# Attention bias added by VectorE out of PSUM, instead of six PE products a head

## What is computed

```python
q, k, v = jnp.split(h @ w_qkv, 3, axis=-1)
# per head, with q as 256 rows
s_own = jnp.einsum('hqd,hkd->hqk', qq, k_own) * scale
dist_own = t[:, None] - (own * B_BLOCK + key_off)[None, :]
s_own = jnp.where((dist_own >= 0)[None],
                  s_own + table_hb[h3, t5_bucket(dist_own)], -jnp.inf)
p = jax.nn.softmax(scores, axis=-1)
out = jnp.einsum('hqk,hkd->hqd', p_own, v_own)
```

## Time and profile before

| what | value |
|---|---|
| median of 3 runs | 1198.73 us (1198.47 to 1199.32) |
| profiled execution, its own time | 1199.04 us |
| its span, first to last instruction | 1197.1 us |
| mean granted TensorE clock | 0.997 |
| busy: PE, DVE, ACT, POOL | 98%, 66%, 56%, 2% |

### The profile page before, as it was taken

One profiled execution on the slowest core, in us unless ns is written; L12 is line 12 of the kernel. 1 busy time (PEld: TensorE's weight loads), 2 busy tenths in 40 slices (PEclk: granted clock), 3 DMA queues, 4 the chain that ended last, 5 costly groups with the idle time before them and its releaser, 6 DMA issues.

```text
span 1197.1 us, 17229 instructions
## 1 busy us (share of the span) xinstructions
PE 1173.2 (98%) x6884; PEld 1038.2 (87%) x6884; DVE 791.3 (66%) x803; ACT 673.4 (56%) x793; POOL 25.9 (2%) x28
## 2 busy tenths in 40 slices
PE   6999999999999999999998999999999999999998
PEld 5999998888889989888887888888898999888886
DVE  6787777655657556755655875656688777755663
ACT  6955675554455444544454754455687567454453
POOL 3000000000001000000000000000000000000000
PEclk9999999999999999999999999999999999999999
DMA  9543335645456434555644545646444333555450
GB/s 348 167 141 106 106 109 180 244 171 199 151 214 212 141 106 169 199 195 177 217 167 141 211 176 200 215 147 210 141 141 142 106 106 109 183 205 208 162 206 35
DMA packets 85128, 202.38 MB, mean 169 GB/s; under 512 B 3293, under 2 KB 5415, under 8 KB 84816
## 3 DMA queue, kind: packets, MB, share of 16 engines
q1 hardware_dynamic: 85040, 201.58, 48.8%
q0 software_dynamic: 32, 0.02, 0.0%
HBM read 200.52 MB, written 1.06 MB: 168 GB/s over the span
## 4 chain that ended last, share of the span: by engine, by line
PE 92%; ACT 3%; DVE 2%; issue 1%; POOL 1%; DMA 1%; SPq 0%; DVEq 0%; ACTq 0%
PE misc L615 10%; PE hb L615 10%; PE acc L667 10%; PE acc L668 10%; PE acc L669 10%; PE hb L620 5%; PE misc L620 5%; PE hb L542 4%; PE hb L543 4%; PE hb L540 4%; PE acc L778 2%; PE hb L557 2%; PE hb L555 2%; PE hb L556 2%; PE acc L766 1%; PE acc L767 1%
## 5 line engine op out<-in xcount | busy, mean ns | idle before, releaser
L1412 DVE TENSOR_TENSOR wlo<-raw,whi 128x2048 fp32r<-128x2048 f32 x186 | 423.4, 2304 | 163.9 <-ACT whi L1032 163.7
L1032 ACT ACTIVATE whi<-raw 128x2048 fp32r<-128x2048 f32 x186 | 348.3, 1906 | 117.5 <-PE acc L669 101.1
L667 PE MATMUL acc<-whi,arena_r 128*128 128x512 f32 x512 | 199.9, 390 | 0.0
L668 PE MATMUL acc<-wlo,arena_r 128*128 128x512 f32 x512 | 199.5, 390 | 0.0
L669 PE MATMUL acc<-whi,arena_r 128*128 128x512 f32 x512 | 199.2, 389 | 0.0
L615 PE MATMUL misc<-xhl,whi 128*128 128x512 f32 x512 | 122.7, 390 | 1.4 <-DVE arena L1863 1.4
L615 PE MATMUL hb<-xhl,whi 128*128 128x512 f32 x512 | 122.7, 390 | 0.0
L615 PEld LDWEIGHTS misc<-xhl,whi 128*128 128x128 f32 x512 | 95.3, 188 | 21.4 <-DVE arena L1863 2.0
L669 PEld LDWEIGHTS acc<-whi,arena_r 128*128 128x128 f32 x512 | 96.1, 188 | 20.2
L667 PEld LDWEIGHTS acc<-whi,arena_r 128*128 128x128 f32 x512 | 96.2, 188 | 19.1
L668 PEld LDWEIGHTS acc<-wlo,arena_r 128*128 128x128 f32 x512 | 96.2, 188 | 18.9
(11 more groups left out here) (263 smaller groups left out, 1810.5 us busy)
## 6 DMA issues: line engine op xcount, KB each, us to landing
raw<-in_mlp_w_dram SPq DMA_DIRECT2D x128, 1024.0 KB, 5.3
raw<-in_a_w_in_dram SPq DMA_DIRECT2D x32, 1024.0 KB, 5.8
raw<-in_b_w_qkv_dram SPq DMA_DIRECT2D x12, 1024.0 KB, 7.4
raw<-in_a_w_out_dram SPq DMA_DIRECT2D x8, 1024.0 KB, 5.1
raw<-in_b_w_out_dram SPq DMA_DIRECT2D x4, 1024.0 KB, 5.1
arena<-in_x_dram SPq DMA_DIRECT2D x2, 512.0 KB, 4.7
arena<-in_decay_dram SPq DMA_DIRECT2D x1, 1024.0 KB, 11.9
arena<-bias_rows SPq DMA_DIRECT2D x1, 1024.0 KB, 6.9
```

What stands on the lines that cost most here:

```text
L667: pe.matmul(o, ys, h, start=first and kt == 0, stop=False, skip_group_check=True)
L668: pe.matmul(o, ys, l, start=False, stop=False, skip_group_check=True)
L1032: act.activation(whi[:, g % 2, u, 0:n], raw[:, g % 2, u, 0:n], ACT.Copy).then_inc(hi_done, 1)
L1412: dve.tensor_tensor(wlo[:, g % 2, u, 0:n], raw[:, g % 2, u, 0:n], whi[:, g % 2, u, 0:n].bitcast(F32), ALU.subtract).then_inc(lo_done, 1)
```

## The change

The bias is no longer multiplied in. DVE adds it while it moves the scores from PSUM to `probs`, and maxima and exponentials then read `probs` in SBUF. The six products a head, `bh`, `bl`, the flip and the identity in fp32r go, with POOL's three instructions and DVE's and ACT's one each that made them. The bias row becomes 1024 long: the row as before, and the same row reversed ahead of it, so a second DVE copy. SP reads three tables of 128x128 a head (two through the row, one through the reversed part; rows of 512 bytes) where it read one of 128x256 (rows of 1 KB): two for the outer thirds of the scores, which DVE reads backwards, and one for the middle third, placed in `hn` (hence a wait for the norm's column sums). PE's `s_step(h)` waits for DVE's adds of head h-2 where it waited for ACT's exponentials, and ACT's wait for `p_mm` moves to DVE.

```diff
-        bias = carve(6144, HEADS, SEQ)
-        bh = arena_r[:, 0:2048].rearrange("p (a b) -> p a b", a=HEADS)
-        bl = arena_r[:, 2048:4096].rearrange("p (a b) -> p a b", a=HEADS)
+        bias_back = carve(6144, HEADS, 2, P)
+        bias_own = hn[:, 0:4, :].rearrange("p a (b x) -> p (a b) x", b=2)
...
                         sp.wait_ge(bias_out, 16)
-                        sp.dma_start(bias, bass.AP(tensor=bias_dram.tensor, offset=0,
-                                                   ap=[[1, P], [2 * SEQ, HEADS], [1, SEQ]])).then_inc(bias_in, 16)
+                        sp.wait_ge(ms_mm, mix_norm(layer) + 1)
+                        for to, first in ((bias_back[:, :, 0, :], SEQ - P + 1), (bias_back[:, :, 1, :], 2 * SEQ + P),
+                                          (bias_own, 2 * SEQ)):
+                            sp.dma_start(to, bass.AP(tensor=bias_dram.tensor, offset=first,
+                                                     ap=[[1, P], [4 * SEQ, HEADS], [1, P]])).then_inc(bias_in, 16)
...
-                        if h == 0:
-                            pe.wait_ge(bl_done, 1)
                         if h >= 2:
-                            pe.wait_ge(sexp, 2 * (h - 1))
-                        pe.matmul(s[:, 0:P], flip[:, :], bh[:, h, P:SEQ], start=True, stop=False)
-                        pe.matmul(s[:, 0:P], flip[:, :], bl[:, h, P:SEQ], start=False, stop=False)
-                        pe.matmul(s[:, 0:P], qT[:, h, 0:P], kT[:, h, 0:P], start=False, stop=True)
...
+                            pe.wait_ge(s_read, h - 1)
+                        pe.matmul(s[:, 0:P], qT[:, h, 0:P], kT[:, h, 0:P], start=True, stop=True)
+                        mm = pe.matmul(s[:, P:3 * P], qT[:, h, P:SEQ], kT[:, h, :], start=True, stop=True,
                                        skip_group_check=True)
...
                     def softmax(h):
                         act.wait_ge(smax, h + 1)
-                        if h >= 2:
-                            act.wait_ge(p_mm, h - 1)
...
-                            ins = act.activation(probs[:, h % 2, cs], acc[h % 2][:, cs], ACT.Exp,
+                            ins = act.activation(probs[:, h % 2, cs], probs[:, h % 2, cs], ACT.Exp,
...
-                        if k == 2:
-                            act.wait_ge(bias_in, 16)
-                            act.activation(bh, bias, ACT.Copy).then_inc(bh_done, 1)
...
-            dve.wait_ge(pool_const, 6)
+            dve.wait_ge(pool_const, 4)
...
-                    ch.did(dve.tensor_copy(bias_row, acc[2][0:HEADS, :]), bias_row_sb)
+                    ch.did(dve.tensor_copy(bias_row[:, 2 * SEQ:4 * SEQ], acc[2][0:HEADS, :]))
+                    ch.did(dve.tensor_copy(bias_row[:, 0:2 * SEQ], acc[2][0:HEADS, ::-1]), bias_row_sb)
...
                         if h >= 2:
+                            dve.wait_ge(p_mm, h - 1)
+                        ch.settle()
+                        if h == 0:
+                            dve.wait_ge(bias_in, 16 * 3)
+                        for_outer = [w.rearrange("p (c x) -> p c x", c=3)[:, 0:3:2, :]
+                                     for w in (probs[:, h % 2, :], acc[h % 2][:, 0:3 * P])]
+                        ch.did(dve.tensor_tensor(for_outer[0], for_outer[1], bias_back[:, h, :, ::-1], ALU.add))
+                        ch.did(dve.tensor_tensor(probs[:, h % 2, P:2 * P], acc[h % 2][:, P:2 * P], bias_own[:, h, :], ALU.add),
+                               s_read)
+                        if h >= 2:
                             dve.wait_ge(sexp, 2 * (h - 1))
-                            ch.settle()
-                        ch.did(dve.tensor_reduce(small[:, k:k + 1], acc[h % 2][:, 0:P], AX.X, ALU.max))
-                        ch.did(dve.tensor_reduce(small[:, k + 1:k + 2], acc[h % 2][:, P:3 * P], AX.X, ALU.max))
+                        ch.settle()
+                        ch.did(dve.tensor_reduce(small[:, k:k + 1], probs[:, h % 2, 0:P], AX.X, ALU.max))
+                        ch.did(dve.tensor_reduce(small[:, k + 1:k + 2], probs[:, h % 2, P:3 * P], AX.X, ALU.max))
...
-                        if k == 2:
-                            dve.wait_ge(bh_done, 1)
-                            ch.did(dve.tensor_tensor(bl, bias, bh.bitcast(F32), ALU.subtract), bl_done)
```

More of the change, by code:

```diff
@@ L188, in build_decoder @@
         tab = sb("tab", [BUCKETS + 1, HEADS])
-        flip = sb("flip", [P, P], F32R)
-        ident_r = sb("ident_r", [P, P], F32R)
         def carve(at, *dims):
@@ L239, in halves @@
                            ap=[list(flat.ap[0]), [2 * m, 256 // m], [step, 2], [1, m]])
-        bias = carve(6144, HEADS, SEQ)
-        bh = arena_r[:, 0:2048].rearrange("p (a b) -> p a b", a=HEADS)
-        bl = arena_r[:, 2048:4096].rearrange("p (a b) -> p a b", a=HEADS)
+        bias_back = carve(6144, HEADS, 2, P)
+        bias_own = hn[:, 0:4, :].rearrange("p a (b x) -> p (a b) x", b=2)
         probs = carve(8192, 2, 3 * P)
         pT = carve(9216, HEADS, 3 * P)
-        flip_in = carve(12416, P)
-        bias_row = arena[0:HEADS, 12288:12800]
+        bias_row = arena[0:HEADS, 11776:12800]
         gain_rows = arena[0:74, 12288:12288 + P]
@@ L269, in build_decoder @@
         misc = [misc_pair[:, i, :] for i in range(2)]
-        bias_dram = nc.dram_tensor("bias_rows", [HEADS, 2 * SEQ], F32, kind="Internal").ap()
+        bias_dram = nc.dram_tensor("bias_rows", [HEADS, 4 * SEQ], F32, kind="Internal").ap()
         raw_in = [[sem(f"raw_in{p}{u}") for u in range(2)] for p in range(2)]
@@ L300, in build_decoder @@
             sem("ol_done"))
-        bias_row_mm, bias_row_sb, bias_out, bias_in, bh_done, bl_done = (
-            sem("bias_row_mm"), sem("bias_row_sb"), sem("bias_out"), sem("bias_in"), sem("bh_done"), sem("bl_done"))
+        bias_row_mm, bias_row_sb, bias_out, bias_in, s_read = (
+            sem("bias_row_mm"), sem("bias_row_sb"), sem("bias_out"), sem("bias_in"), sem("s_read"))
         s_mm, smax, sexp, sscaled, p_mm, p_sb = (sem("s_mm"), sem("smax"), sem("sexp"), sem("sscaled"),
@@ L883, in _ @@
                     pe.wait_ge(tab_in, 32)
-                    pe.wait_ge(pool_const, 6)
+                    pe.wait_ge(pool_const, 4)
                     pe.wait_ge(y_sb, 4 * (layer - 1) + 3)
@@ L890, in s_step @@
                         pe.wait_ge(bank_free, free_count(layer) + 4 * (h // 4 + 1))
-                        if h == 0:
-                            pe.wait_ge(bl_done, 1)
                         if h >= 2:
-                            pe.wait_ge(sexp, 2 * (h - 1))
-                        pe.matmul(s[:, 0:P], flip[:, :], bh[:, h, P:SEQ], start=True, stop=False)
-                        pe.matmul(s[:, 0:P], flip[:, :], bl[:, h, P:SEQ], start=False, stop=False)
-                        pe.matmul(s[:, 0:P], qT[:, h, 0:P], kT[:, h, 0:P], start=False, stop=True)
-                        own = slice(SEQ - 1, P - 1, -1)
-                        pe.matmul(s[:, P:2 * P], ident_r[:, :], bh[:, h, 0:P], start=True, stop=False,
-                                  skip_group_check=True)
-                        pe.matmul(s[:, P:2 * P], ident_r[:, :], bl[:, h, 0:P], start=False, stop=False,
-                                  skip_group_check=True)
-                        pe.matmul(s[:, 2 * P:3 * P], ident_r[:, :], bh[:, h, own], start=False, stop=False,
-                                  skip_group_check=True)
-                        pe.matmul(s[:, 2 * P:3 * P], ident_r[:, :], bl[:, h, own], start=False, stop=False,
-                                  skip_group_check=True)
-                        mm = pe.matmul(s[:, P:3 * P], qT[:, h, P:SEQ], kT[:, h, :], start=False, stop=True,
+                            pe.wait_ge(s_read, h - 1)
+                        pe.matmul(s[:, 0:P], qT[:, h, 0:P], kT[:, h, 0:P], start=True, stop=True)
+                        mm = pe.matmul(s[:, P:3 * P], qT[:, h, P:SEQ], kT[:, h, :], start=True, stop=True,
                                        skip_group_check=True)
@@ L1933, in _ @@
             ch.settle()
-            ch.did(pool.memset(flip_in, 0.0))
-            ch.settle()
             ch.did(pool.affine_select(out=ident[:, :], in_=ident[:, :], compare_op=ALU.not_equal, fill=1.0, base=0,
@@ L1943, in _ @@
             ch.did(pool.memset(tab[BUCKETS:BUCKETS + 1, :], MASKED), pool_const)
-            ch.settle()
-            ch.did(pool.affine_select(out=flip_in, in_=flip_in, compare_op=ALU.not_equal, fill=1.0, base=1 - P,
-                                      pattern=[[1, P]], channel_multiplier=1))
-            ch.settle()
-            ch.did(pool.tensor_copy(flip[:, :], flip_in), pool_const)
-            ch.did(pool.tensor_copy(ident_r[:, :], ident[:, :]), pool_const)
             def sum_squares(n):
```

## The result

| | before | after |
|---|---|---|
| median, same chip | 1199.03 us (1198.47 to 1199.35, 4 runs) | 1206.93 us (1206.47 to 1207.31, 4 runs) |
| ratio after / before | | 1.0064, 95% interval 1.0052 to 1.0077 |
| profiled execution, its span | 1199.04, 1197.1 us | 1206.47, 1204.4 us |
| mean granted TensorE clock | 0.997 | 0.993 |

The kernel became 0.64% slower, past the upper end of the range (1201.0). Lines have moved in the changed kernel: ACT's split is L1018, VectorE's L1393, the adds L1742 and L1743, maxima L1748 and L1749, exponentials L1266, the copy of the transposes L1272, scores L892 and L893, transposes L902, SP's loads L403 and its table reads L432.

What follows compares the result with a forecast made beforehand. PE, busy 98% of the span, bounds the kernel; after the change the ACT and DVE chain binds attention. -2.0 us (chain) + 1.5 (clock) = -0.5: 1198.5 us for the profiled execution, median 1198.2, range 1195.0 to 1201.0.

Steps and rivals of the forecast that it cites:

- The three loads: SP's table reads before attention: cost the weight unit behind them 3.5 us, landing at 377.7, still hidden.
- The slower rival: The tables' packets delay group 3's first unit; 1201.0 us at the packets' bound; chance 0.18.
- two more issues of 0.37 us: On SP's queue, the added table loads' issues only queue behind data still moving; cost put at nothing.
- past 378.68 each microsecond would delay the whole chain: At ACT's split of group 3's first unit: later landing delays early maxima and, after 0.3 us slack, the chain.
- the clock: After PE's 2.8 us wait near the attention stage's end, a lower granted clock costs 1.5 us, bounds 0 and 1.7.
- the chain becomes the bound: In attention, ACT and DVE's loop takes 6.96 us a head against PE's 6.6 to 6.8; gain 2.0 us.
- The choice of no change for reductions: DVE's maxima cost the same from SBUF as from PSUM; the other bound saved 0.07 us on each of two.
- The second rival: Chain bound with the clock kept: 1196.7 us (1195.8 to 1197.1); chance 0.13.
- what comes off PE: Six bias products a head in attention: 0.60 us, at most 0.66; 4.8 us over eight heads.
- It doesn't stall PE at first: In attention PE runs on despite the slower chain, and the lag collects at the end as a 2.8 us wait.

Runs made afterwards that it cites:

- Experiment 5: The changed kernel with neighbouring heads' bias rows 2 KB apart in DRAM instead of 4 KB, still three table loads: 1200.25 us, ratio 1.0011.
- Experiment 6: The kernel before with its heads 4 KB apart in DRAM instead of 2 KB, nothing else: 1200.39 us, ratio 1.0012.
- experiments 3: The changed kernel with all table reads aligned (partition step 0 in DRAM, bias wrong): 1207.2 us, ratio 1.0072.
- experiment 4: The changed kernel with the three table loads issued from ACT's queue instead of SP's: 1203.4 us, ratio 1.0035.
- experiment 2: The kernel before with its one table load cut into two of 512 B rows, same bytes: 1198.94 us, ratio 0.9999.
- experiment 9: The changed kernel, heads still 4 KB apart, with VectorE's adds and maxima put ahead of its weight split: 1195.68 us, ratio 0.9973.
- experiment 8: The changed kernel with heads 2 KB apart and VectorE's adds and maxima put ahead of its weight split: 1193.77 us, ratio 0.9957.
- experiment 1: The changed kernel loading only the middle table, which all adds read (bias wrong): 1199.59 us, ratio 1.0004.
- experiment 7: The changed kernel with only the middle table (bias wrong), plus 15 filler products on PE before the last transposes: 1197.09 us, ratio 0.9984.
- 10: The changed kernel, heads 2 KB apart, maxima ahead of the split, table reads issued between group 3's two weight units: 1194.28 us, ratio 0.9959.

## Why the prediction was wrong

**The step that failed is "The three loads".** Their cost to the unit behind was put at 3.5 us, with 1.9 and 7.6 as bounds; it was 10.6. The slower rival, given 0.18, thus had the mechanism and its threshold right, and the size wrong. Experiment 5 has everything of the change but the distance between heads: its unit landed at 379.9, 5.7 us later than before, inside the bounds. The other 5 us came from the distance, which the prediction did not look at: it read bytes, rows and alignment off the diff and passed over `2 * SEQ` turning into `4 * SEQ`. Experiment 6 shows that term without the rest (the unit takes 2.7 us longer), experiments 3 and 5 together rule out alignment, and experiment 4 rules out that only SP's held-up issue was at fault. That issue, 3.38 us where two took 0.99, was missed as well: "two more issues of 0.37 us". So was 0.4 us for the write: twice as long, it landed 2.3 us after its issue instead of 1.9, and SP issued the reads at 365.15 instead of 364.70. Why rows 4 KB apart move at half the rate is not shown by these runs.

By the Trainium skill (DMA: Bandwidth & Descriptors, Specifications) rows of 512 B would have gone by bytes. The measurement decides against it for these overlapping reads of a small region: 74 to 86 GB/s at 4 KB between heads and 174 to 179 at 2 KB, while the 1 KB rows of before, with the unit behind them, moved at 246 to 349. At 2 KB experiment 2 comes close to it all the same, with 1.3 us for twice the rows.

**What the lateness cost was the order's doing.** The prediction said that past 378.68 each microsecond would delay the whole chain. That held: 6.2 us late at the split, and head 7's sums were read at 440.14 instead of the forecast's 433.75, 6.4 us late. With 1.1 us more for the clock than forecast (below), that makes 7.5 of the 8.0 us between the forecast for the profiled execution, 1198.5, and its 1206.47; the rest is not attributed. But the prediction took VectorE's order as given. Experiments 9 and 8 show the other half: with the maxima ahead of the split, the 4 KB between heads cost 1.8 us, 1.1 of them PE's wait for the late unit in experiment 9's trace, instead of 6.5 (the changed kernel against experiment 5).

**Right: the chain becomes the bound.** Forecast 6.96 us a head, measured 6.98 (experiments 1 and 7, and the changed kernel); adds 0.42 and 0.28, the maxima at 128 and 256 elements 0.29 and 0.41 from SBUF. The choice of no change for reductions was the right end: by the Trainium skill (VectorE: DVE Perf Modes, section on the TRN2 errata) they should have cost less each, an estimate of 0.07 us from its fixed parts, and these rows show none of it. Without the extra loads and with the clock kept the gain was 1.7 us (experiment 7: 1197.09 against 1198.83), forecast 2.0 with 1.7 as the lower bound. The second rival, chain bound and clock kept, was priced at 1196.7 (1195.8 to 1197.1), and this kernel is its case, at the upper end.

**Right, at its bound: what comes off PE.** In the changed kernel the scores of heads 0 and 1 stand 6.41 us apart, against 7.07: 0.66, the upper bound, not 0.60. Where PE is the slower party nearly all of it comes through: 8 x 0.66 = 5.3 us, and experiment 8 gains 5.1. The 0.5 us beyond the forecast's 4.8 also lengthen PE's wait where the chain binds: 3.5 us in experiment 1, forecast 2.8.

**Wrong size: the clock.** Forecast 1.5 us with 1.7 as the upper bound, measured 2.2 by the medians and 2.6 by the traces (experiment 1 against 7). In experiment 1 the rows read 0.78, 0.50 and 0.59 over 9 us, a longer stretch than the 4 and 3 us of the earlier trace rows on which the bound stood. So even with the loads priced well the sum would have come out above before, as experiment 1 did by 0.4, not 0.5 below.

**Missed: the bank.** "It doesn't stall PE at first" held only while the lag was under the 2.2 us of slack between the emptying of the projection bank and head 4's scores. In the changed kernel PE stopped there for 2.71 us, and the clock was low from 414 to 417. The projections that followed were not the slower party then, and the next copy came 7.19 us after the last instead of 6.98, so it cost 0.2 us; it was a second sign of the same lag, not a second cause.

The balance in the two profiles: the last copy of the stage ended at 442.35 instead of 437.69, 4.7 us later, and from there to ACT's last rounding of the outputs it took 8.3 us instead of 5.7 (450.68 and 443.40), 2.6 more, with the clock low: together the 7.3 us between the spans.

## What to carry to other kernels

Before pricing an operation that is added to an engine's chain, look at what stands ahead of it in that engine's program and whether it needs it: here a swap of two calls was worth 11 us in the kernel as changed, more than the change itself in either direction. When a diff touches an access pattern, compare every stride of it, not only bytes and row lengths, and count the issuing queue's own time. A gain off the bounding engine comes through only as far as the next chain has slack; add up both loops per head, and if the new one is longer, reorder it first.

## What the runs showed of the hardware that was not expected

- Reads of 512 B rows from DRAM moved at 74 to 86 GB/s with 4 KB between the rows of neighbouring heads (63 to 75 for the one table of experiment 1), and at 174 to 179 with 2 KB. With 1 KB rows the same change of distance took a 1 MB read from 6.9 to 9.5 us.
- A DMA's issue can hold its queue: two reads of 1024 rows were issued in 0.99 us, the third took 3.38 us on SP (4.37 with aligned reads, 1.95 at 2 KB, 4.72 at 2 KB behind a weight unit) and 6.43 on ACT's queue.
- The clock does not fall after every wait of a given length. The same wait of PE in layer 2, 2.49 and 2.48 us, is followed by 0.50 from 656 to 658 us in experiment 9 and by 1.00 from 652 to 662 us in experiment 8. After the same wait the clock was kept in the profiled executions of experiments 7 and 10 too, and was low in those of the kernel before, the changed one, and experiments 1, 3, 5 and 6. What decides it stays open, and differences of a microsecond between single executions can come from it.
